# Attention's values as the stationary operand, two query blocks in two halves of the columns, the results turned back by transposes

## What is computed

```python
for window, dil in ((128, 1), (512, 4), (2048, 16)):      # 8 heads of 64
    o, l = _dilated_prompt_cfg(qa, ka, va, rel_bias, window, dil)
    ...
# one (window, dilation): blocks of 128 queries against their own and the previous block of keys
s = q @ k.T * ATTN_SCALE + bias;  s = where(mask, s, -inf)
m = max(s);  p = exp(s - m);  den = sum(p)
out = (p / den) @ v;  lse = m + log(den)
...
attn = sum(softmax(lses) * outs)                          # the three dilations merged
a_out = attn * silu(ga);  y = LayerNorm(ALPHA * x + concat(a_out, b_out) @ w_out)
```

## Time and profile before

| | us |
|---|---|
| runs: median of 3 (lowest to highest) | 1592.22 (1588.28 to 1593.67) |
| profiled execution, its own time | 1593.84 |
| its span in the trace | 1592.0 |
| PE, PEld busy | 1531.7 (96%), 1374.3 (86%) |
| DVE, ACT, POOL busy | 767.2 (48%), 503.4 (32%), 440.9 (28%) |
| attention's window, 1070 to 1375 us: PE, DVE, ACT, POOL busy | 297.76, 222.03, 216.56, 241.06 |
| value products (L1784), 1200 instructions: PE, PEld busy | 157.7, 150.1 |

### The profile page before, as it was taken

How to read it: one execution, slowest core, us unless ns; L and a number is a source line. 1 busy time by engine, 2 the same in 40 slices (tenths; PEclk the granted TensorE clock), 3 DMA queues, 4 the chain that set the end, 5 groups by cost and what they waited for, 6 DMA issues and landing times. The chain is left out here.

```text
span 1592.0 us, 25593 instructions
## 1 busy us (share of the span) xinstructions
PE 1531.7 (96%) x9830; PEld 1374.3 (86%) x9830; DVE 767.2 (48%) x1941; ACT 503.4 (32%) x1426; POOL 440.9 (28%) x281
## 2 busy tenths in 40 slices
PE   7999999998999999899998999989899999899998
PEld 7999999996788777677787999979899999788886
DVE  6022110004323224121214699847677777698885
ACT  5111111113200114122322032337677777423321
POOL 1233210000330000000001000018987779344443
PEclk9999999998999999999999599989999999999999
DMA  9999996233786957866665547859696971866642
GB/s 308 338 329 350 343 318 187 81 117 124 210 291 191 313 200 261 299 213 207 202 205 140 114 157 220 257 185 236 138 207 150 202 183 63 286 207 214 219 158 78
DMA packets 174501, 338.34 MB, mean 213 GB/s; under 512 B 15635, under 2 KB 115283, under 8 KB 165523
## 3 DMA queue, kind: packets, MB, share of 16 engines
q1 hardware_dynamic: 141452, 169.18, 35.0%
q10 hardware_dynamic: 22432, 111.29, 22.0%
q0 software_dynamic: 10512, 56.48, 13.3%
HBM read 262.25 MB, written 155.39 MB: 262 GB/s over the span
## 5 line engine op out<-in xcount | busy, mean ns | idle before, releaser
L1394 POOL CAST a_sorted<-a_plain 128x2048 fp32r<-128x2048 f32 x45 | 171.6, 3872 | 240.5 <-POOLq L932 204.8
L251 PE MATMUL acc<-xhi,whi 128*128 128x424 f32 (+1 forms) x640 | 227.3, 355 | 8.6 <-DVE xlo L230 8.6
L759 PE MATMUL nacc<-nwhi,nxhi 128*128 128x512 f32 (+1 forms) x544 | 219.5, 403 | 13.5 <-DVE nwlo L494 7.3
L251 PE MATMUL acc<-xlo,whi 128*128 128x424 f32 (+1 forms) x640 | 226.9, 355 | 0.0
L251 PE MATMUL acc<-xhi,wlo 128*128 128x424 f32 (+1 forms) x640 | 226.8, 354 | 0.0
L759 PE MATMUL nacc<-nwlo,nxhi 128*128 128x512 f32 (+1 forms) x544 | 214.5, 394 | 0.0
L759 PE MATMUL nacc<-nwhi,nxlo 128*128 128x512 f32 (+1 forms) x544 | 214.5, 394 | 0.0
L1659 ACT ACTIVATE a_prob<-a_prob,a_stage 128x256 f32<-128x256 f32 (+1 forms) x384 | 174.1, 454 | 84.2 <-DVE a_stage L1501 81.9
L1501 DVE CUSTOM_DVE_ANT_0 a_prob<-a_banks,a_bias 128x256 f32<-128x256 f32 (+1 forms) x384 | 125.4, 364 | 82.0 <-PE a_banks L1759 73.5
L1784 PE MATMUL a_banks<-a_v,a_probT 128*128 128x64 f32 x1200 | 157.7, 269 | 4.4 <-DVE a_probT L1513 4.4
L1784 PEld LDWEIGHTS a_banks<-a_v,a_probT 128*128 128x128 f32 x1200 | 150.1, 193 | 5.8 <-DVE a_probT L1513 5.0
(11 more groups left out here) (215 smaller groups left out, 2547.3 us busy)
## 6 DMA issues: line engine op xcount, KB each, us to landing
a_plain<-split_qk POOLq DMA_DIRECT2D x48, 512.0 KB, 12.5
out_kwin_s<-in_cache_kT ACTq DMA_DIRECT2D x8, 2048.0 KB, 19.3
split_qk<-spare POOLq DMA_DIRECT2D x16, 1024.0 KB, 14.6
spare<-in_xT SPq DMA_DIRECT2D x32, 512.0 KB, 7.1
projN<-nstage SPq DMA_DIRECT2D x32, 512.0 KB, 6.6
qg<-in_cache_kT ACTq DMA_DIRECT2D x8, 2048.0 KB, 10.6
kf<-in_cache_v ACTq DMA_DIRECT2D x8, 2048.0 KB
out_kwin_s<-in_cache_kT ACTq DMA_DIRECT2D x8, 2032.0 KB, 28.6
```

What stands on the lines that cost most here:

```text
L251: mm = pe.matmul(acc[:, j, 0:n], w[:, u, k], x[:, k, c0:c0 + n], start=(k == 0 and a == 0), stop=(k == KD - 1 and a == 2))
L759: mm = pe.matmul(acc[0:m, n % 2], x[:, u, k, 0:m], w[:, k, g * H:(g + 1) * H], start=(k == 0 and b == 0), stop=(k == KD - 1 and b == 2))
L1394: nc.gpsimd.tensor_copy(dst[:, n].rearrange("p (r m) -> p r m", r=d), src[:, n].bitcast(F32).rearrange("p (m r) -> p r m", r=d)).then_inc( ...
```

## The change

`values` swaps its operands: the values [128 keys, 64] are stationary and the turned probabilities [128 keys, 128 queries] are streamed. The result is [64, 128 queries]; the block w = 0 goes to partitions 0 to 63 of the PSUM bank (column half 0 of the array) and w = 1 to 64 to 127 (column half 1), and the tiles are issued so that the halves alternate. A bank then holds a group of four units, [2 x 64, 4 x 128 queries]. ACT copies it to a new SBUF tile `oT` (`keep_turned`), PE transposes it back in four 128x128 pieces into the same bank (`turn_back`), which gives the layout of before, and ACT evacuates it as before, now waiting for `back_done`. The last group's `turn_back` stands inside `project(0)`, and its `evacuate` after `recurrent_part(1)`.

```diff
--- before.py
+++ after.py
@@ -1217,6 +1217,7 @@
         stage = sb("a_stage", [P, NC, NBK, 2, OW])
         prob = sb("a_prob", [P, 4, 2, 2 * P])
         probT = sb("a_probT", [P, 3, 4, P])
+        oT = sb("a_oT", [P, 4, P])
         bias.append(sb("a_bias1", [P, 2, NC, 2 * P]))
         v.append(sb("a_v1", [P, NC, NBK, P]))
         sorted_.append(sb("a_sorted2", [P, 3, T], F32R))
@@ -1228,6 +1229,7 @@
         s_done, p_done, e_done, t_done, pt_done, pv_done, o_out, sort_done = (
             sem(f"a_{n}") for n in ("s_done", "p_done", "e_done", "t_done", "pt_done", "pv_done", "o_out", "sort_done"))
         pair_landed, bias_landed, const = keep["pair_landed"], keep["bias_landed"], keep["const"]
+        ot_done, back_done = sem("a_ot_done"), sem("a_back_done")
         NLD = 6
 
         slices = [t[:].rearrange("p n t -> p (n t)").rearrange("p (m a d) -> p m a d", m=3, a=2)
@@ -1660,9 +1662,15 @@
                                                    accum_out=to[:, DA:DA + 1])
                     ins.then_inc(e_done, 1)
 
+                def keep_turned(m):
+                    act.wait_ge(pv_done, 4 * (m + 1))
+                    if m >= 1:
+                        act.wait_ge(back_done, m)
+                    nc.scalar.activation(oT[:].rearrange("p j d -> p (j d)"), o_ps[:, m % 2], ACT.Copy).then_inc(ot_done, 1)
+
                 def evacuate(n):
                     h, c, b = units[n]
-                    act.wait_ge(pv_done, n + 4)
+                    act.wait_ge(back_done, n // 4 + 1)
                     nc.scalar.activation(stage[:, c, b:b + 8, h % 2, 0:DA],
                                          o_ps[:, (n // 4) % 2].rearrange("p (b d) -> p b d", d=DA), ACT.Copy).then_inc(o_out, 1)
 
@@ -1713,16 +1721,19 @@
                 for n in range(NU + 5):
                     if n < NU:
                         exponential(n)
-                    if n >= 8 and n % 4 == 0:
-                        evacuate(n - 8)
+                    if n == NU + 3:
+                        round_mix(0)
+                    if n >= 7 and n % 4 == 3:
+                        keep_turned(n // 4 - 1)
+                    if n >= 9 and n % 4 == 1:
+                        evacuate(n - 9)
                     if n == HU * (HALVES - 1):
                         sample_squares()
                     if n == NU - 1:
                         recurrent_part(0)
-                    if n == NU + 3:
-                        round_mix(0)
                 dilation_weights(1)
                 recurrent_part(1)
+                evacuate(NU - 4)
                 for i in range(1, LAST + 2):
                     if i + 1 < NALL:
                         dilation_weights(i + 1)
@@ -1779,12 +1790,18 @@
                     if n % 4 == 0 and n >= 8:
                         pe.wait_ge(o_out, n // 4 - 1)
                     ts = tiles(c, b)
-                    for a, (w, vt, _) in enumerate(ts):
-                        col = (2 * (n % 4) + w) * DA
-                        mm = pe.matmul(o_ps[:, (n // 4) % 2, col:col + DA], probT[:, n % 3, a],
-                                       v[g % 2][:, c, vt, x * DA:(x + 1) * DA],
-                                       start=(a == 0 or ts[a - 1][0] != w), stop=(a == len(ts) - 1 or ts[a + 1][0] != w))
+                    first_of = [next(a for a, t in enumerate(ts) if t[0] == w) for w in range(2)]
+                    for a, (w, vt, _) in sorted(enumerate(ts), key=lambda t: (t[0] - first_of[t[1][0]], t[1][0])):
+                        mm = pe.matmul(o_ps[w * DA:(w + 1) * DA, (n // 4) % 2, n % 4 * P:(n % 4 + 1) * P],
+                                       v[g % 2][:, c, vt, x * DA:(x + 1) * DA], probT[:, n % 3, a],
+                                       start=(a == first_of[w]), stop=(a == len(ts) - 1 or ts[a + 1][0] != w))
                     mm.then_inc(pv_done, 1)
+
+                def turn_back(m):
+                    pe.wait_ge(ot_done, m + 1)
+                    for j in range(4):
+                        mm = pe.transpose(o_ps[:, m % 2, j * P:(j + 1) * P], oT[:, j], ident[:])
+                    mm.then_inc(back_done, 1)
 
                 def transposes(p):
                     n, u = rows_in[p], p % 2
@@ -1809,6 +1826,8 @@
                     if p >= 2:
                         pe.wait_ge(zr, p - 1)
                     for k in range(KD):
+                        if k == 4 and p == 0:
+                            turn_back(NU // 4 - 1)
                         if k == 4 and 1 <= p < LAST:
                             transposes(p + 1)
                         whi, wlo = w_parts(k)
@@ -1843,6 +1862,8 @@
                         turn(n - 2)
                     if n >= 4:
                         values(n - 4)
+                    if n >= 9 and n % 4 == 1:
+                        turn_back(n // 4 - 2)
                 project(0)
                 transposes(1)
                 pe.wait_ge(o_out, NU // 4)
```

## The result

The changed kernel takes 1618.5 us, the median of 4 runs (1604.7 to 1620.0), beside 1590.3 us for the kernel before (1588.2 to 1593.7, 4 runs). The ratio is 1.0154, with a 95% interval of 1.0129 to 1.0178, so the change costs about 25 us; the two medians differ by 28. The forecast was 1616.5, in a range of 1597 to 1636, with 0.88 on slower. The time is right, but none of the three terms is: PE's stream was forecast at 23.4 us and came out at 18.1, the stall that I had set to nothing is 5.9, and the tail is 3.1 instead of 0.9.

A forecast was written before the change was run, and what follows sets the result against it. The prediction took TensorE (PE) to bound the kernel. A longer PE stream (+23.4 us) and a later last evacuation (+0.9) gave +24.3 on the median of 1592.22, about 1616.5 us, range 1597 to 1636.

The forecast's parts named there:

- PE's stream: TensorE's work in the attention up to the last units: switches and transposes back, less halved products, add 23.4 us.
- the stall: DVE's wait for a store of partials, 4.7 us at the third head before: no net change.
- the tail: After the last units, the evacuation of group 45 waits for turn_back and starts 0.9 us later against TensorE's work.
- Two halves at once: Value products in the two column halves overlap, so a unit takes 4 or 2 steps of 0.109 us.
- a toll of 0.35 for entry and exit: Each unit's switch into half-width products and out again costs 0.34 us, 0.35 with the other half's lag.
- bound that I kept: Limits for switches no row shows: from nothing up to waiting out 0.27 us, +0.07 on each of 384, +27 us.
- (a): The column halves run one after the other in the values, some 62 us over 192 units: 1676 us; chance 0.08.
- (b): No switching cost between these array shapes, so the values save 63 us: about 1556 us; chance 0.07.
- (d): Smaller switching cost at one of two crossings only, some 0.1 us a unit, -20 us: 1597 us; chance 0.10.
- The sum of units: Value products with switches over 192 units: -9.7, +4.6 and +7.7 us for units of 8, 6 and 4, together +2.6.
- turn_back, 0.436 each: Four fp32 transposes at 0.109 us after each group of four units; 47 in the unit loop add 20.5 us.
- (c): Draining lets TensorE's clock fall to 1.2 GHz in part of the attention: 1650 us and more; chance 0.03.

The follow-up runs named there:

- the swap alone: The changed kernel without turn_back and keep_turned, so the attention's results stay turned: 1593.76 us, 1.0034 of the kernel before.
- pairs: The changed kernel with the values of two units issued together, in every second iteration of PE: 1585.08 us, 0.9966 of the kernel before.
- small loads: Kernels before and after, each loading only 128 of 2048 columns of q and k for heads 2 to 7: 1584.35 and 1604.75 us.

## Why the prediction was right, and where it was not

**PE's stream is the bound.** Right. The head is 38.50 of 38.50 us PE, and ACT's copies are hidden (0.2 us of idle time ahead of L1669).

**Two halves at once, 0.109 a step, a toll of 0.35 for entry and exit.** Right: wide units -0.11, units of dilation 16 +0.12 (forecast -0.110 and +0.120), and the toll by itself 0.33. Neither bound that I kept was near: the transposes with 64 columns of the earlier trace rows aren't a model for fp32 products with 64, and no switch waits out a full 0.27. (Half of the upper bound gives 1630, not the 1632 that I wrote, so the range should have ended 2 us lower.) Rivals (a), (b) and (d) fall with it: the value instructions enter behind a hole, as forecast, and run two at a time. The rows of L783 and L784, the same shape and data type elsewhere in the kernel, were the right place to read.

The Trainium skill, TensorEngine Tiling (Array Packing), section Key Properties, has the drain on a change of mode, and the trace of the kernel after agrees: a hole of 0.17 us in the weight loads at each; only the transposes with 64 columns of the earlier trace rows show none. Its recommendation in When to Use Tiling, a 2x column tiling after the swap, holds here inside a group only (4 steps instead of 8), and the switches around each group eat it: +0.13 us a head with a group per unit, and a gain with two units a group.

**The sum of units.** Mis-sized, by little: 0.33 us a head forecast, 0.13 measured. The three prices were right; I had taken every unit of the kernel before to be free of waits, and one in each of the four heads without a stall (the fourth to the seventh) isn't.

**turn_back, 0.436 each.** Mis-sized: 0.39. I took four steps of a stream of transposes. It stands at the exit from the halves, behind the same hole as scores would, and from its first load to that of the scores behind it the four loads take 0.39 us. Times 47 it is 18.3 us instead of 20.5. Up to the end of the stretch, 46 of them are 17.9 us where I had 20.1, and that leaves 0.2 us for the units where I had 3.3: together +18.1 for 23.4.

**The stall, "no net change".** Wrong in the mechanism, and the largest miss: +5.9 us between the profiled executions. I asked how far the store and the block that needs it slide, found 1 us, and left the stall where it was. I didn't ask what it would cost elsewhere. Rival (c) had the right quantity, a clock that falls to 1.2 GHz within the stage, with the wrong cause: not the drains, but a wait of under 4 us in front of units of dilation 16. The kernel before with such a wait at that place loses 11.2 us as well.

**The tail, +0.9.** Too small: +3.1. Timeline of the kernel after, around what was 1361.92 in the earlier trace rows, and combine(0) of the kernel before:

```profile
1384.11 2.40 DVE L1553 TENSOR_TENSOR m_mix<-a_v,a_bias 64x512 f32<-64x512 f32 x1
1385.31 0.42 PEld L1803 LDWEIGHTS a_banks<-a_ident,a_oT 128*128 128x128 f32 x4 [0.17 <-issue]
1387.23 0.51 ACT L1661 ACTIVATE a_prob<-a_prob,a_stage 128x256 f32<-128x256 f32 x1 [2.52 <-DVE a_stage L1503]
1388.23 0.58 ACT L1674 ACTIVATE a_stage<-a_banks 128x512 f32<-128x512 f32 x1
```
```profile
1361.40 1.22 DVE L1551 TENSOR_TENSOR m_mix<-a_v,a_bias 64x512 f32<-64x512 f32 x1
```

turn_back was loaded at 1385.31, where I had it. But its evacuation comes at 1388.23. It is issued one iteration later than before, and so stands behind exponential(189) on ACT; that waits for DVE's minima, and these for combine(0), which took 2.40 us instead of 1.22. Against the end of iteration 189 the evacuation went from 0.69 us ahead to 2.54 behind, 3.2 us, and the tail grew by 3.1. I had read the wait that was added, but not who is now queued ahead of the waiting instruction.

The two causes can be told apart. In the runs with the swap alone and with pairs combine(0) took 0.67 us only; there the evacuation stands 1.2 us behind the end of the iteration, 1.9 later than before, and the tail grew by 2.0 and 2.5. So the new order on ACT is the larger part, and the length of combine(0) the rest. That length goes with POOL, which splits the last weights at this time. POOL before, POOL after, and DVE with pairs:

```profile
1361.04 1.04 POOL L1400 CAST m_late_w<-a_wraw 128x1024 fp32r<-128x1024 f32 x1 [6.56 <-DMA a_wraw<-in_w_o]
```
```profile
1383.59 2.38 POOL L1404 TENSOR_TENSOR m_late_w<-a_wraw,m_late_w 128x1024 fp32r<-128x1024 f32 x1
```
```profile
1351.96 0.67 DVE L1553 TENSOR_TENSOR m_mix<-a_v,a_bias 64x512 f32<-64x512 f32 x1
```

Started beside an instruction of POOL that was under way, combine(0) ended 0.54 us after that one did (1362.62 and 1362.08 before, 1386.51 and 1385.97 after); started ahead of POOL's, it took 0.67.

**The sum.** Stream -5.3, stall +5.9, tail +2.2, start -0.9 against my terms: 1.9 us in all between the spans, 26.2 for 24.3. That the forecast was nearer than its parts is luck: the stream's error and the stall's cancel. Had the stall stayed away, as in the kernels with small loads, the change would have cost 20.4 us.

## What to carry to other kernels

Price a change of array shape by its switches, not by its products: here a switch in and out costs 0.33 us, as much as three steps of a value instruction, so groups of four or six instructions lose and groups of eight win little, and the same edit with two units a group (turning back included) is 5 us faster than the kernel before. Grouping ends where the engines that feed the group run dry. And when an edit shifts the work past a wait on DMA, ask not only whether the wait grows but what follows it: a standstill of 3 to 4 us cost 7.5 us in one place and 11 to 13 in another.

## What the runs showed of the hardware that I had not expected

- After a stall, how long TensorE stayed at 1.2 GHz depended on the place: the clock was back 3 to 7 us after PE went on in dilation 1 and 19 to 22 us in dilation 16, with PE busy in full both times and in both kernels. A stall of 3.3 us was enough for 17.1 us of low clock.
- A DVE product of 128x1536 fp32 took 1.76 us while POOL was idle, 4.4 to 5.2 us beside POOL's sort, and 10.99 us once, over three of POOL's instructions. In the kernels before with a stall made by hand, each of the longer ones ended 1.62 us after an instruction of POOL did, as if it had waited for POOL and then run by itself; combine(0) shows the same with 0.54.
- A store of 528 KB took 18.6 to 20.9 us to land while a load in 8 KB packets ran on another queue.
- Two halves of the columns overlap in whatever order their products are issued (38.57 and 38.49 us a head); the starts come in pairs, 0.013 us apart, even where a whole half is issued ahead of the other.
